# A two-layer decoder trunk on one Trainium2 core: the first weight pieces in halves, gains applied to the transposed x, and broadcasts and lambda sums later on GpSimd

## The chip, the cores and the metric

The kernel runs on one core of a Trainium2 chip. The metric is the device time of one execution in microseconds (us), as the median of several runs. Positions in a trace are us from the start of the profiled span. TensorE is called PE in the rows, VectorE DVE, ScalarE ACT, GpSimd POOL and SyncE SP.

## The reference

x has 256 rows of 1024 float32. Two layers, each a half-step FFN, a mixer, and a second half-step FFN, and a last RMSNorm:

```python
for l in range(2):
    x = x + 0.5 * swiglu(rmsnorm(x, norm_ffn1[l]), w1_gate[l], w1_up[l], w1_down[l])
    h = rmsnorm(x, norm_mix[l])
    dq, dk, dv, rq, rk, rv, rg = split(h @ w_in[l])
    lam = (exp(sum(lambda_q1[l] * lambda_k1[l])) - exp(sum(lambda_q2[l] * lambda_k2[l])) + lam_init)
    ...
    x = x + concat(o_diff, o_ret) @ w_out[l]
    x = x + 0.5 * swiglu(rmsnorm(x, norm_ffn2[l]), w2_gate[l], w2_up[l], w2_down[l])
return rmsnorm(x, norm_final)
```

Left out are `o_diff`, differential attention with `lam` (4 heads), and `o_ret`, retention (4 heads). `rmsnorm(x, g)` is x / sqrt(mean(x^2) + 1e-6) * g, `swiglu` is (silu(x @ gate) * (x @ up)) @ down with an inner width of 2816.

## The kernel before, in words

**Precision.** Every matmul of weights is done three times. A weight piece (128 x 2048 float32, 1 MB) is loaded into one of three `raw` slots. ScalarE rounds it into `w_hi` (`split_hi`, L329), VectorE takes the rest, raw minus `w_hi`, into `w_lo` (`split_lo`, L536); both have six slots. TensorE then adds hi*hi, hi*lo and lo*hi (`three`, L798 to L800). The activations are split in the same way (`xT_hi`, `xT_lo` for the transposed x).

**Entry of a block** (number q, seven in all, the last being the output). x is held in two row tiles of 128 rows, tt = 0 and 1. For each, VectorE adds the accumulators to x (`residual`, L569), multiplies by `gain` into `wide` (L572), TensorE transposes `wide` into the PSUM tiles `tp` (`enter_T`, L813), ScalarE copies them to `xT_hi` (L354), VectorE subtracts into `xT_lo` (L553). ScalarE also sums the squares (`squares`, L349), and GpSimd makes the factor `rstd` from them in two small steps (`entry`, L226 and L228). `rstd` is applied after the projection, so the projection doesn't wait for it. `gain` holds one norm's weights, broadcast to all partitions; GpSimd reloads it after each entry (`next_gain`, 0.5 MB).

**FFN.** Eleven steps of 256 columns. A step has two `up` calls (one for each row tile, 24 matmuls with gate and up side by side in `gu[tt]`) and two `down` calls, which run one step behind. Between them the hidden tile is turned by way of memory: ScalarE silu (L372), VectorE product with `rstd` (`hide`, L595), GpSimd copy that takes the 16-bit halves apart (`turn_out`, L246), a transposing DMA triggered by ScalarE (`turn`, L377), GpSimd copy back (`turn_back`, L252), ScalarE and VectorE split (L382, L553). `up` number e waits for `hidden_done` e - 1, since two PSUM tiles are used in turn.

**What sets the order.** Each engine runs a program written out by hand and waits on counting semaphores. ScalarE's in a step are these:

```python
silu(s_, 0, it, pos)
nxt(0)
turn(d, 0)
silu(s_, 1, it, pos)
nxt(1)
turn(d + 1, 1)
```

where `nxt` splits a piece and `turn` begins with a wait for `halves_done` of GpSimd's copy. SyncE issues the weight loads in order; a load waits until the piece three before has been split.

**The start.** SyncE loads the first half of x (L160) and the pieces from L173; ScalarE triggers the gain broadcast (L509); GpSimd makes the identity, issues five broadcasts (four lambda vectors L279, diff_subln L280), makes the tables `bias8` and `decay`, then the two factors. ScalarE triggers the load of the second half of x only once piece 0 has landed (`act.wait_ge(raw_loaded[0], 32)`, L514, L515), and splits pieces 0 and 1 after that. VectorE sums the lambda products (L767).

Of the kernel before, what the change touches and what calls it, by code (L numbers as in the profile page):

```python
# [21 lines left out]
P = 128  # L22
D, SEQ, DEPTH = 1024, 256, 2
TT = SEQ // P
KT = D // P
# [28 lines left out]
def build(nc, x_in, norm_ffn1, w1_gate, w1_up, w1_down, norm_mix, w_in, lam_q1, lam_k1, lam_q2, lam_k2,  # L54
          subln, w_out, norm_ffn2, w2_gate, w2_up, w2_down, norm_final, out):
    ctx = ExitStack()
    with ctx:
# [16 lines left out]
        gain = sb("gain", [P, D])  # L74
# [27 lines left out]
        dq_dk = wide  # L102

# [8 lines left out]
        def retT(h, a, b):  # L112
# [11 lines left out]
        gain0_loaded = sem("gain0_loaded")  # L124
# [6 lines left out]
        acc_ready, x_new, xg_ready, sq_done, rstd_done, xT_psum, xT_hi_done, xT_lo_done = (  # L131
            sem(n) for n in ("acc_ready", "x_new", "xg_ready", "sq_done", "rstd_done", "xT_psum", "xT_hi_done", "xT_lo_done"))
# [25 lines left out]
        def _(sp):  # L158
# [16 lines left out]
            def ffn(layer, base, wg, wu, wd):  # L175
# [5 lines left out]

                def load_down(it, pos, j):
                    load(layer, it, base + pos, [wd[layer, bass.ds(j * CH + k * P, P), :] for k in range(2)])

                load_gu(0, 0, 0)
# [33 lines left out]
        def _(pool):  # L219
            def load_gain(src):  # L220
                pool.dma_start(gain[:, :], src.partition_broadcast(P)).then_inc(gain_loaded, 16)

# [14 lines left out]

            def next_gain(q, src):
                pool.wait_ge(xg_ready, 4 * q + 4)
                load_gain(src)  # L240
# [46 lines left out]
            for h in range(HEADS):  # L287
                nc.gpsimd.tensor_scalar(bias8[:, h, :], bias8[:, h, :], -SLOPES[h] / SCALE, None, ALU.mult).then_inc(pool_steps, 1)
            pool.wait_ge(decay_exp, HEADS)
            nc.gpsimd.tensor_scalar(decay[:, :, :], decay[:, :, :], SCALE, None, ALU.mult).then_inc(pool_steps, 1)  # L290
            pool.wait_ge(pool_steps, 5 + HEADS + DEPTH)
            nc.gpsimd.affine_select(out=bias8[:, :, :], in_=bias8[:, :, :], compare_op=ALU.is_ge, fill=MASKED, base=P,
                                    pattern=[[0, HEADS], [-1, SEQ]], channel_multiplier=1).then_inc(consts_made, 1)
            nc.gpsimd.affine_select(out=decay[:, :, :], in_=decay[:, :, :], compare_op=ALU.is_ge, fill=0.0, base=0,
                                    pattern=[[0, HEADS], [1, SEQ]], channel_multiplier=-1).then_inc(consts_made, 1)
            for tt in range(TT):
                entry(0, tt)
            next_gain(0, norm_mix[0, :])

            def mixer_and_ffn2_entry(layer):  # L300
                for tt in range(TT):
                    entry(3 * layer + 1, tt)
                next_gain(3 * layer + 1, norm_ffn2[layer, :])
# [7 lines left out]
            for layer in range(DEPTH):  # L311
                if layer:
                    for tt in range(TT):
                        entry(3 * layer, tt)
                    next_gain(3 * layer, norm_mix[layer, :])
                ffn(layer, 0)
                mixer_and_ffn2_entry(layer)
                next_gain(3 * layer + 2, norm_ffn1[layer + 1, :] if layer < DEPTH - 1 else norm_final[:])
                ffn(layer, 1)
# [5 lines left out]
        def _(act):  # L325
# [4 lines left out]

            def ahead(layer, pos, some=range(AHEAD)):

                for p_ in some:
                    split_hi(layer, pos + p_)
# [9 lines left out]
            def squares(q, tt):  # L344
                if isinstance(q, int) and q == 0:
                    act.wait_ge(x_loaded[tt], 16)
                else:
                    act.wait_ge(x_new, 4 * (q - 1) + 2 * tt + 2)
                nc.scalar.activation(junk.bitcast(BF16)[:, tt * D:(tt + 1) * D], x[:, tt, :], ACT.Square, accum_out=ssq[:, tt:tt + 1]).then_inc(sq_done, 1)  # L349

            def xT_parts(q, tt):
                for half in range(2):
                    act.wait_ge(xT_psum, 4 * q + 2 * tt + half + 1)
                    nc.scalar.activation(xT_hi[:, 4 * half:4 * half + 4, tt * P:(tt + 1) * P],  # L354
                                         tp[half][:, :].rearrange("p (k n) -> p k n", k=4), ACT.Copy).then_inc(xT_hi_done, 1)
# [83 lines left out]
            def mixer(layer):  # L439
# [33 lines left out]
                act.wait_ge(lam_steps, 2 * DEPTH)  # L473
# [35 lines left out]
            act.dma_start(gain[:, :], norm_ffn1[0, :].partition_broadcast(P)).then_inc(gain0_loaded, 16)  # L509
# [7 lines left out]
            for tt in range(TT):  # L517
                squares(0, tt)
            xT_parts(0, 1)
            with act.Fori(0, DEPTH) as layer:  # L520
# [12 lines left out]
        def _(dve):  # L533
# [4 lines left out]

            def ahead(layer, pos, some=range(AHEAD)):

                for p_ in some:
                    split_lo(layer, pos + p_)
# [12 lines left out]
            def residual(q, tt, factor, used):  # L555

                if factor is None:
                    dve.wait_ge(x_loaded[tt], 16)
                    dve.wait_ge(gain0_loaded, 16)
                else:  # L560
                    dve.wait_ge(gain_loaded, 16 * q)
                for half in range(2):
                    cols = slice(half * 512, (half + 1) * 512)
                    if factor is not None:
                        if (tt, half) != (1, 1):
                            dve.wait_ge(acc_ready, 3 * (q - 1) + 2 * tt + half + 1)
                        else:
                            dve.wait_ge(slot_free, SLOTS + used)
                        nc.vector.scalar_tensor_tensor(x[:, tt, cols], acc[2 * tt + half][:, :], factor, x[:, tt, cols],  # L569
                                                       ALU.mult, ALU.add).then_inc(x_new, 1)  # L570
                        dve.wait_ge(x_new, 4 * (q - 1) + 2 * tt + half + 1)
                    nc.vector.tensor_tensor(wide[:, tt, cols], x[:, tt, cols], gain[:, cols], ALU.mult).then_inc(xg_ready, 1)  # L572

            def xT_parts(q, tt):
                for half in range(2):
                    dve.wait_ge(xT_hi_done, 4 * q + 2 * tt + half + 1)
                    ks = slice(4 * half, 4 * half + 4)
                    lo_of(xT_lo[:, ks, tt * P:(tt + 1) * P], tp[half][:, :].rearrange("p (k n) -> p k n", k=4),
                          xT_hi[:, ks, tt * P:(tt + 1) * P], xT_lo_done)

            def enter(q, factor, used):
                for tt in range(TT):
                    residual(q, tt, factor, used)
                    xT_parts(q, tt)
# [172 lines left out]
            residual(0, 0, None, 0)  # L757
            xT_parts(0, 0)
            ahead(0, 0)
            residual(0, 1, None, 0)  # L760
            xT_parts(0, 1)
            dve.wait_ge(lam_loaded, 16 * 5)

            for l in range(DEPTH):
                for m in range(2):
                    cols = slice(l * QK, (l + 1) * QK)
                    nc.vector.tensor_tensor_reduce(out=gate[:, 0, (2 * l + m) * QK:(2 * l + m + 1) * QK], in0=lams[:, 2 * m, cols],  # L767
                                                   in1=lams[:, 2 * m + 1, cols], scale=1.0, scalar=0.0, op0=ALU.mult, op1=ALU.add,
                                                   accum_out=lam_dot[:, 2 * l + m:2 * l + m + 1]).then_inc(lam_steps, 1)
            for l in range(DEPTH):  # L770
                nc.vector.tensor_scalar(gsub2[:, l, :], gsub2[:, l, :], 1.0 - LAM_INIT[l], None, ALU.mult).then_inc(lam_steps, 1)
            with dve.Fori(0, DEPTH) as layer:
                ffn(layer, 0, 0)
                dve.wait_ge(lam_steps, 3 * DEPTH)

                nc.vector.tensor_copy(gsub[:, :], gsub2[:, bass.ds(layer, 1), :].rearrange("p l n -> p (l n)")).then_inc(layer_vals, 1)
                enter(3 * layer + 1, 0.5, LP * layer + MIX0)
                mixer(layer)
                enter(3 * layer + 2, 1.0, LP * layer + FFN2)
                ffn(layer, 1, FFN2)  # L780
                with dve.If(layer < DEPTH - 1):
                    enter(3 * layer + 3, 0.5, LP * layer + LP)
            q = 3 * DEPTH
            for tt in range(TT):
                residual(q, tt, 0.5, LP * DEPTH)
            for tt in range(TT):
                dve.wait_ge(rstd_done, TT * q + tt + 1)
                dve.wait_ge(xg_ready, 4 * q + 2 * tt + 2)
# [261 lines left out]
```

## Time and profile before

| | |
|---|---|
| median of 3 runs | 977.25 us (976.73 to 977.7) |
| the profiled execution | 975.21 us |
| its span | 973.4 us |
| PE busy | 944.2 us, 97% |
| DVE, ACT, POOL busy | 557.0, 460.7, 195.0 us |
| granted clock, mean | 0.998 |
| read from memory | 177.08 MB |

The span is the profiled part of the execution, 1.8 us shorter than the execution's own time. Busy time of an engine is the time its instructions cover; a wait of an engine is the gap before an instruction, with the releaser that ended it. The start and the turns from one block to the next are the places where TensorE may stand.

### The profile page before, as it was taken

The numbers are of one execution on the slowest core, as the hardware profiler recorded it, in microseconds if no ns is written. First come the engines' busy times: TensorE is split into PE (matmuls) and PEld (weight loads), VectorE is DVE, ScalarE is ACT, GpSimd is POOL, SyncE is SP. The second block draws the span as 40 slices with busy tenths as digits, with TensorE's granted clock in tenths as the row PEclk, the third lists the DMA queues.
The fourth block names the chain that finished last, engine by engine and source line by source line (L and its number), as shares of the span: only waits on it lengthen the run. The fifth ranks groups of instructions, "written<-read, shape, count | busy, mean of one in ns | idle before, by whom it ended". The sixth has DMA issues, their size and how long they took to land.

```text
span 973.4 us, 13400 instructions
## 1 busy us (share of the span) xinstructions
PE 944.2 (97%) x4352; PEld 781.8 (80%) x4352; DVE 557.0 (57%) x628; ACT 460.7 (47%) x579; POOL 195.0 (20%) x233
## 2 busy tenths in 40 slices
PE   2999999999999999999989999999999999999996
PEld 2888888888888888888878888888888888888885
DVE  3555555665576565555645656466665756555554
ACT  4544444545574444444454444344656545444441
POOL 7133211100010323131013311210001024212210
PEclk9999999999999999999999999999999999999999
DMA  9787777546345786666638867665624646867641
GB/s 253 211 233 212 209 226 226 188 162 213 113 148 173 205 244 204 216 200 220 223 112 233 231 196 217 204 214 190 228 97 172 211 126 215 249 191 227 193 143 43
DMA packets 166699, 189.19 MB, mean 194 GB/s; under 512 B 49184, under 2 KB 139296, under 8 KB 166656
## 3 DMA queue, kind: packets, MB, share of 16 engines
q1 hardware_dynamic: 121808, 173.56, 54.3%
q10 hardware_dynamic: 43808, 11.54, 6.8%
q0 software_dynamic: 1040, 3.54, 1.3%
q8 instruction: 23, 0.38, 0.2%
q14 instruction: 20, 0.16, 0.1%
HBM read 177.08 MB, written 1.05 MB: 183 GB/s over the span
## 4 chain that ended last, share of the span: by engine, by line
PE 95%; DMA 1%; ACT 1%; DVE 1%; issue 1%; SPq 0%; ACTq 0%; POOLq 0%; DVEq 0%; POOL 0%
PE gu L798 21%; PE gu L800 21%; PE gu L799 21%; PE acc L800 10%; PE acc L798 10%; PE acc L799 10%; DMA raw<-in_w_up_dram 1%; PE tp L813 1%; PE tp L912 1%; PE acc L923 1%; PE tp L935 1%; DVE w_lo L536 0%; ACT w_hi L329 0%; ACT wide L452 0%; PE acc L935 0%
## 5 line engine op out<-in xcount | busy, mean ns | idle before, releaser
L536 DVE TENSOR_TENSOR w_lo<-raw,w_hi 128x2048 fp32r<-128x2048 f32 (+1 forms) x168 | 383.0, 2284 | 164.3 <-ACT w_hi L329 163.8
L798 PE MATMUL gu<-w_hi,xT_hi 128*128 128x512 f32 x896 | 352.4, 393 | 13.0 <-DVE w_lo L536 10.5
L800 PE MATMUL gu<-w_hi,xT_lo 128*128 128x512 f32 x896 | 349.5, 390 | 0.0
L799 PE MATMUL gu<-w_lo,xT_hi 128*128 128x512 f32 x896 | 349.5, 390 | 0.0
L329 ACT ACTIVATE w_hi<-raw 128x2048 fp32r<-128x2048 f32 (+1 forms) x168 | 313.0, 1867 | 21.6 <-DMA raw<-in_w_up_dram 10.9
L798 PEld LDWEIGHTS gu<-w_hi,xT_hi 128*128 128x128 f32 x896 | 168.7, 188 | 49.3 <-issue 12.9
L800 PEld LDWEIGHTS gu<-w_hi,xT_lo 128*128 128x128 f32 x896 | 168.6, 188 | 35.5
L799 PEld LDWEIGHTS gu<-w_lo,xT_hi 128*128 128x128 f32 x896 | 168.8, 188 | 34.2
L798 PE MATMUL acc<-w_hi,aT_hi 128*128 128x512 f32 x384 | 150.8, 393 | 0.0
L800 PE MATMUL acc<-w_hi,aT_lo 128*128 128x512 f32 x384 | 149.6, 390 | 0.0
L799 PE MATMUL acc<-w_lo,aT_hi 128*128 128x512 f32 x384 | 149.4, 389 | 0.0
L372 ACT ACTIVATE hid<-gu,st 128x256 f32<-128x256 f32 x88 | 41.6, 473 | 219.3 <-PE gu L800 186.9
L246 POOL COPY kT<-hid 128x512 uint16<-128x512 uint16 x80 | 60.6, 757 | 332.1 <-DVE hid L595 332.1
L252 POOL COPY qT<-kT 128x512 uint16<-128x512 uint16 x80 | 97.0, 1219 | 125.1 <-issue 88.3
L595 DVE SCALAR_TENSOR_TENSOR hid<-gu,st,hid 128x256 f32<-128x256 f32 x88 | 42.4, 482 | 123.2 <-ACT hid L372 123.1
L382 ACT ACTIVATE aT_hi<-qT 128x256 fp32r<-128x256 f32 x80 | 33.4, 417 | 133.4 <-POOL qT L252 133.4
L800 PEld LDWEIGHTS acc<-w_hi,aT_lo 128*128 128x128 f32 x384 | 72.1, 188 | 15.2
L799 PEld LDWEIGHTS acc<-w_lo,aT_hi 128*128 128x128 f32 x384 | 72.2, 188 | 14.7
L798 PEld LDWEIGHTS acc<-w_hi,aT_hi 128*128 128x128 f32 x384 | 72.1, 188 | 14.4
L553 DVE TENSOR_TENSOR aT_lo<-qT,aT_hi 128x256 fp32r<-128x256 f32 x80 | 35.0, 438 | 46.1 <-ACT aT_hi L382 46.1
L354 ACT ACTIVATE xT_hi<-tp 128x512 fp32r<-128x512 f32 x24 | 13.2, 596 | 61.0 <-PE tp L813 61.0
L226 POOL TENSOR_SCALAR st<-st 128x1 f32<-128x1 f32 x14 | 3.8, 274 | 179.3 <-ACT rT L349 179.2
(115 smaller groups left out, 406.8 us busy)
## 6 DMA issues: line engine op xcount, KB each, us to landing
raw<-in_w_gate_dram SPq DMA_DIRECT2D x88, 512.0 KB, 4.0
raw<-in_w_up_dram SPq DMA_DIRECT2D x88, 512.0 KB, 5.0
raw<-in_w_down_dram SPq DMA_DIRECT2D x88, 512.0 KB, 3.9
raw<-in_w_in_dram SPq DMA_DIRECT2D x40, 512.0 KB, 4.7
raw<-in_w_out_dram SPq DMA_DIRECT2D x16, 512.0 KB, 3.6
raw<-in_w_in_dram SPq DMA_DIRECT2D x16, 256.0 KB, 2.8
gain<-in_norm_ffn_dram POOLq DMA_DIRECT2D x3, 512.0 KB, 3.7
kT<-kT ACTq DMA_TRANSPOSE x80, 3.3
```

The lines of the kernel that those rows point to most:

```text
L246: nc.gpsimd.tensor_copy(halves[:, tt, :, :], hidden[:, tt, :].bitcast(U16).rearrange("p (n h) -> p h n", h=2)).then_inc(halves_done, 1)
L252: nc.gpsimd.tensor_copy(hidT[:, tt, :].bitcast(U16).rearrange("p (n h) -> p h n", h=2), halvesT[:, tt, :, :]).then_inc(hidT_done, 1)
L329: nc.scalar.activation(w_hi[:, pos % SLOTS, 0:n], raw[:, pos % RAW, 0:n], ACT.Copy).then_inc(hi_done, 1)
L354: nc.scalar.activation(xT_hi[:, 4 * half:4 * half + 4, tt * P:(tt + 1) * P], tp[half][:, :].rearrange("p (k n) -> p k n", k=4), ACT.Copy). ...
L372: nc.scalar.activation(silu_g[:, tt, :], gu[tt][:, 0:CH], ACT.Silu, scale=rstd[:, tt:tt + 1]).then_inc(silu_done, 1)
L382: nc.scalar.activation(aT_hi[:, 2 * par:2 * par + 2, tt * P:(tt + 1) * P], hidT[:, tt, :].rearrange("p (k n) -> p k n", k=2), ACT.Copy).th ...
L536: nc.vector.tensor_tensor(w_lo[:, pos % SLOTS, 0:n], raw[:, pos % RAW, 0:n], w_hi[:, pos % SLOTS, 0:n].bitcast(F32), ALU.subtract).then_in ...
L553: nc.vector.tensor_tensor(dst, src, hi.bitcast(F32), ALU.subtract).then_inc(done, 1)
L595: nc.vector.scalar_tensor_tensor(hidden[:, tt, :], gu[tt][:, CH:2 * CH], rstd[:, tt:tt + 1], silu_g[:, tt, :], ALU.mult, ALU.mult).then_in ...
L798: nc.tensor.matmul(out_, s_hi, m_hi, start=first, stop=False)
L799: nc.tensor.matmul(out_, s_hi, m_lo, start=False, stop=False)
L800: return nc.tensor.matmul(out_, s_lo, m_hi, start=False, stop=last)
```

## The change

- **Weights.** Pieces 0 and 1 of each layer's first FFN are loaded in two halves of 1024 columns (`load_first`), each with its own semaphore, and split in halves by ScalarE and VectorE (`split_first_hi`, `split_first_lo`). TensorE waits for `lo_half` ahead of the first two of a piece's four row blocks, for `lo_done` ahead of the third.
- **Gains.** The three norms' weights (two layers each) are loaded as 48 rows of 128 (24 KB), transposed once by TensorE, and kept as `gT`, one column for each 128 values. TensorE transposes x itself; VectorE multiplies the transposed tile in PSUM by `gT` into `wide`, and the hi and lo parts are made from `wide`. The output norm's gain alone is still a broadcast, into `gate`, loaded once.
- **GpSimd.** The five small broadcasts are issued after the two factors of the first entry. The lambda sums are made there by a product and six halving additions, and `gsub2` is scaled there.
- **ScalarE at the start.** The squares of row tile 1 come after its `xT_parts`.

```diff
+                def load_first():
+                    for pos in range(AHEAD):
+                        sp.wait_ge(lo_done, LP * layer + pos + 1)
+                        for part, loaded in enumerate((half_loaded, raw_loaded)):
...
+                            for g, w in enumerate((wg, wu)):
+                                rows = slice(pos * 512 + part * 256, pos * 512 + (part + 1) * 256)
+                                sp.dma_start(dst[:, :, g, :], w[layer, rows, 0:CH].rearrange("(k p) n -> p k n", p=P)).then_inc(loaded[pos], 16)
...
-            for i, lam in enumerate((lam_q1, lam_k1, lam_q2, lam_k2)):
-                pool.dma_start(lams[:, i, :], lam.rearrange("l n -> (l n)").partition_broadcast(P)).then_inc(lam_loaded, 16)
-            pool.dma_start(gsub2[:, :, :].rearrange("p l n -> p (l n)"),
-                           subln.rearrange("l n -> (l n)").partition_broadcast(P)).then_inc(lam_loaded, 16)
...
+            for tt in range(TT):
+                entry(0, tt)
+            for i, lam in enumerate((lam_q1, lam_k1, lam_q2, lam_k2)):
+                pool.dma_start(lams[:, i, :], lam.rearrange("l n -> (l n)").partition_broadcast(P)).then_inc(lam_loaded, 16)
...
+            pool.wait_ge(lam_loaded, 16 * 5)
+            pairs = lams.rearrange("p (m b) (l n) -> p m b l n", b=2, l=DEPTH)
+            dots = pairs[:, :, 0, :, :]
+            nc.gpsimd.tensor_tensor(dots, dots, pairs[:, :, 1, :, :], ALU.mult).then_inc(lam_sums, 1)
+            for i in range(6):
+                n = QK >> (i + 1)
+                dst = dots[:, :, :, 0:n] if n > 1 else lam_dot.rearrange("p (l m n) -> p m l n", m=2, n=1)
+                pool.wait_ge(lam_sums, i + 1)
+                nc.gpsimd.tensor_tensor(dst, dots[:, :, :, 0:n], dots[:, :, :, n:2 * n], ALU.add).then_inc(lam_sums, 1)
+            for l in range(DEPTH):
+                nc.gpsimd.tensor_scalar(gsub2[:, l, :], gsub2[:, l, :], 1.0 - LAM_INIT[l], None, ALU.mult).then_inc(lam_sums, 1)
...
+            def split_first_hi(layer, pos):
+                nth = layer + pos // LP
+                act.wait_ge(half_loaded[pos % LP], 32 * nth + 32)
+                act.wait_ge(slot_free, LP * layer + pos + 1)
+                nc.scalar.activation(w_hi[:, pos % SLOTS, 0:1024], raw[:, pos % RAW, 0:1024], ACT.Copy).then_inc(hi_half, 1)
+                act.wait_ge(raw_loaded[pos % RAW], 32 * (LP // RAW * layer + pos // RAW + 1))
+                nc.scalar.activation(w_hi[:, pos % SLOTS, 1024:PIECE], raw[:, pos % RAW, 1024:PIECE], ACT.Copy).then_inc(hi_done, 1)
...
-            act.dma_start(gain[:, :], norm_ffn1[0, :].partition_broadcast(P)).then_inc(gain0_loaded, 16)
+            for i, norm in enumerate((norm_ffn1, norm_mix, norm_ffn2)):
+                act.dma_start(gain_rows[i * DEPTH * KT:(i + 1) * DEPTH * KT, :],
+                              norm.rearrange("l (k p) -> (l k) p", p=P)).then_inc(gains_loaded, 16)
...
             act.wait_ge(raw_loaded[0], 32)
             act.dma_start(x[:, 1, :], x_in[0, P:2 * P, :]).then_inc(x_loaded[1], 16)
             ahead(0, 0)
-            for tt in range(TT):
-                squares(0, tt)
+            squares(0, 0)
             xT_parts(0, 1)
+            squares(0, 1)
...
+                for half in range(2):
+                    dve.wait_ge(xT_psum, 4 * q + 2 * tt + half + 1)
+                    g = gT[:, bass.ds(col + 4 * half, 4)].unsqueeze(2).broadcast_to([P, 4, P])
+                    nc.vector.tensor_tensor(of(wide, half), tp[half][:, :].rearrange("p (k n) -> p k n", k=4), g, ALU.mult).then_inc(xg_done, 1)
...
-                          xT_hi[:, ks, tt * P:(tt + 1) * P], xT_lo_done)
...
+                    lo_of(xT_lo[:, ks, tt * P:(tt + 1) * P], of(wide, half), xT_hi[:, ks, tt * P:(tt + 1) * P], xT_lo_done)
```

GpSimd's instructions from its first tables to its first copy of a hidden tile (`kT<-hid`), before:

```order
L279 DMA qT<-in_lambda_k_dram 128x128
L280 DMA gsub<-in_diff_subln_dram 128x256
L283 MEMSET st 128x1 x2
L284 IOTA bias 128x1024
L288 TENSOR_SCALAR bias<-bias 128x256 x4
L290 TENSOR_SCALAR decay<-decay 128x1024
L292 AFFINE_SELECT bias<-bias 128x1024
L294 AFFINE_SELECT decay<-decay 128x1024
L226 TENSOR_SCALAR st<-st 128x1
L228 TENSOR_TENSOR st<-st 128x1
```

The second factor, one reload of `gain` (L221) and the copy follow. And with the change, from the second factor's last step on:

```order
L242 TENSOR_TENSOR st<-st 128x1
L301 DMA qT<-in_lambda_q_dram 128x128
L301 DMA qT<-in_lambda_k_dram 128x128
L301 DMA qT<-in_lambda_q_dram 128x128
L301 DMA qT<-in_lambda_k_dram 128x128
L302 DMA gsub<-in_diff_subln_dram 128x256
L305 TENSOR_SCALAR decay<-decay 128x1024
L307 AFFINE_SELECT decay<-decay 128x1024
L312 TENSOR_TENSOR qT<-qT 128x2x128
L317 TENSOR_TENSOR qT<-qT 128x2x2x32
L317 TENSOR_TENSOR qT<-qT 128x2x2x16
L317 TENSOR_TENSOR qT<-qT 128x2x2x8
```

Three more additions, two TENSOR_SCALAR on `gsub2` and then the copy of the first hidden tile (L256) follow. The broadcasts and the work on `decay` moved from ahead of the factors to behind them, and the lambda steps joined them.

ScalarE at the start, before:

```order
L354 ACTIVATE xT_hi<-tp 128x4x128 x2
L515 DMA x<-in_x_dram 128x1024
L329 ACTIVATE w_hi<-raw 128x2048 x2
L349 ACTIVATE rT,st<-x 128x1024 x2
L354 ACTIVATE xT_hi<-tp 128x4x128 x2
```

And with the change:

```order
L386 ACTIVATE xT_hi<-wide 128x4x128 x2
L549 DMA x<-in_x_dram 128x1024
L356 ACTIVATE w_hi<-raw 128x1024
L358 ACTIVATE w_hi<-raw 128x1024
L356 ACTIVATE w_hi<-raw 128x1024
L358 ACTIVATE w_hi<-raw 128x1024
L381 ACTIVATE rT,st<-x 128x1024
L386 ACTIVATE xT_hi<-wide 128x4x128 x2
L381 ACTIVATE rT,st<-x 128x1024
```

The pieces are split in four halves, still behind the load of x's second half, and the second squares moved behind the copies of the second x tile.

## Rows read from the trace of the kernel before

**Rows 1.** Who waited for whom, TensorE: total us, times, longest.

```profile
PE gu L798 <- DVE w_lo L536: 10.5, 1, 10.5
PE tp L813 <- DVE wide L572: 7.3, 1, 7.3
```

**Rows 2.** The chain that ended last, 0 to 26 us: start, duration, what.

```profile
2.15 12.80 DMA raw<-in_w_up_dram
...
15.42 1.92 ACT w_hi L329
...
17.36 2.30 DVE w_lo L536
...
19.80 0.79 PE gu L798
...
24.57 0.87 PE tp L813 x8
```

**Rows 3.** Windows of the start: busy us by engine, clock, DMA share, GB/s.

```profile
0.00:7.00 7.00, 0.00 (x0) 0.00 (x0) 0.53 (x1) 2.62 (x5) 6.05 (x17) 1.00 0.68 214
7.00:15.00 8.00, 1.94 (x8) 1.55 (x8) 2.35 (x4) 1.19 (x2) 7.69 (x7) 1.00 0.96 178
15.00:20.00 5.00, 0.20 (x1) 0.21 (x2) 2.54 (x2) 4.10 (x3) 0.51 (x1) 1.00 1.10 368
```

**Rows 4.** DMA issues, 0 to 40 us: KB each, us from issue to landing.

```profile
x<-in_x_dram ACTq DMA_DIRECT2D x1, 512.0 KB, 7.0
...
gsub<-in_diff_subln_dram POOLq DMA_DIRECT2D x1, 128.0 KB, 10.1
```

**Rows 5.** Timeline, first x tile: start, us, engine, line, operation, [idle before].

```profile
6.47 1.49 DVE L572 TENSOR_TENSOR wide<-x,gain 128x512 f32<-128x512 f32 x2 [6.47 <-DMA x<-in_x_dram]
...
9.29 0.60 ACT L354 ACTIVATE xT_hi<-tp 128x512 fp32r<-128x512 f32 x1 [0.26 <-PE tp L813]
```

**Rows 6.** Timeline of ScalarE from its first table load in layer 1.

```profile
26.15 1.28 ACT L329 ACT_TABLE_LOAD   x1
...
30.68 0.48 ACT L372 ACTIVATE hid<-gu,st 128x256 f32<-128x256 f32 x1
```

**Rows 7.** Timeline of GpSimd, 0 to 36 us.

```profile
2.51 0.75 POOL L279 DMA_DIRECT2D qT<-in_lambda_q_dram  x1
...
4.87 0.55 POOL L280 DMA_DIRECT2D gsub<-in_diff_subln_dram  x1
...
10.52 2.77 POOL L290 TENSOR_SCALAR decay<-decay 128x1024 f32<-128x1024 f32 x1
...
14.46 1.05 POOL L294 TENSOR_SCALAR_AFFINE_SELECT decay<-decay 128x1024 f32<-128x1024 f32 x1
20.84 1.25 POOL L226 TENSOR_SCALAR st<-st 128x1 f32<-128x1 f32 x1 [5.33 <-ACT rT L349]
...
23.19 0.19 POOL L226 TENSOR_SCALAR st<-st 128x1 f32<-128x1 f32 x1
...
32.27 0.60 POOL L246 COPY kT<-hid 128x512 uint16<-128x512 uint16 x1 [7.69 <-DVE hid L595]
```

**Rows 8.** GpSimd's copy back, one line: ns min/median/max.

```profile
L252 POOL COPY qT<-kT x80: 757/770/2919, 38.2 to 941.6; 128x512 uint16<-128x512 uint16 x80
```

**Rows 9.** Groups by form, GpSimd: count, busy us, mean ns, idle before.

```profile
L288 POOL TENSOR_SCALAR bias<-bias 128x256 f32<-128x256 f32 x4 | 3.8, 949 | 0.2
...
L234 POOL TENSOR_SCALAR hn<-hn 128x4 f32<-128x4 f32 x8 | 1.5, 190 | 134.2 <-ACT rT L436 133.8
```

**Rows 10.** Timeline of TensorE: first matmuls of the fourth `up` and of `down`.

```profile
38.91 0.39 PE L798 MATMUL gu<-w_hi,xT_hi 128*128 128x512 f32 x1
...
44.35 0.39 PE L798 MATMUL acc<-w_hi,aT_hi 128*128 128x512 f32 x1
```

**Rows 11.** Timeline of TensorE at the start of layer 2.

```profile
506.38 0.49 PE L798 MATMUL gu<-w_hi,xT_hi 128*128 128x512 f32 x1 [0.74 <-DVE hid L595]
```

**Rows 12.** Timeline of VectorE at the end.

```profile
968.76 0.88 DVE L791 TENSOR_SCALAR x<-wide,st 128x512 f32<-128x512 f32 x2 [0.71 <-POOL st L228]
```

More of the change, by code:

```diff
@@ L537, in split_lo, with split_first_lo @@
                                         w_hi[:, pos % SLOTS, 0:n].bitcast(F32), ALU.subtract).then_inc(lo_done, 1)
+            def split_first_lo(layer, pos):
+                nth = layer + pos // LP
+                for part, when, count, done in ((0, hi_half, AHEAD * nth + pos % LP + 1, lo_half), (1, hi_done, LP * layer + pos + 1, lo_done)):
+                    cs = slice(part * 1024, (part + 1) * 1024)
+                    dve.wait_ge(when, count)
+                    nc.vector.tensor_tensor(w_lo[:, pos % SLOTS, cs], raw[:, pos % RAW, cs], w_hi[:, pos % SLOTS, cs].bitcast(F32),
+                                            ALU.subtract).then_inc(done, 1)
             def ahead(layer, pos, some=range(AHEAD)):
                 for p_ in some:
-                    split_lo(layer, pos + p_)
+                    if pos % LP:
+                        split_lo(layer, pos + p_)
+                    else:
+                        split_first_lo(layer, pos + p_)
             def ahead_after(layer, f, some):
@@ L785, in _ @@
                 residual(q, tt, 0.5, LP * DEPTH)
+                for half in range(2):
+                    cols = slice(half * 512, (half + 1) * 512)
+                    dve.wait_ge(gain_loaded, 16)
+                    dve.wait_ge(x_new, 4 * q + 2 * tt + half + 1)
+                    nc.vector.tensor_tensor(wide[:, tt, cols], x[:, tt, cols], gain[:, cols], ALU.mult).then_inc(xg_done, 1)
             for tt in range(TT):
                 dve.wait_ge(rstd_done, TT * q + tt + 1)
-                dve.wait_ge(xg_ready, 4 * q + 2 * tt + 2)
+                dve.wait_ge(xg_done, 4 * q + 2 * tt + 2)
                 for half in range(2):
@@ L807, in enter_T, with project @@
                 for half in range(2):
-                    pe.wait_ge(xg_ready, 4 * q + 2 * tt + half + 1)
+                    if isinstance(q, int) and q == 0:
+                        pe.wait_ge(x_loaded[tt], 16)
+                    else:
+                        pe.wait_ge(x_new, 4 * q + 2 * tt + half + 1)
                     if tt:
-                        pe.wait_ge(xT_lo_done, 4 * q + half + 1)
+                        pe.wait_ge(xg_done, 4 * q + half + 1)
                     for k in range(4):
                         c = (4 * half + k) * P
-                        ins = nc.tensor.transpose(tp[half][:, k * P:(k + 1) * P], wide[:, tt, c:c + P], ident[:, :])
+                        ins = nc.tensor.transpose(tp[half][:, k * P:(k + 1) * P], x[:, tt, c:c + P], ident[:, :])
                     ins.then_inc(xT_psum, 1)
-            def project(layer, it, tt, pos, n_pieces, ready, hook=None, entry=None):
+            def project(layer, it, tt, pos, n_pieces, ready, hook=None, entry=None, halved=False):
                 kk = KT // n_pieces
@@ L821, in project @@
                     slot = (pos + h) % SLOTS
-                    if tt == 0:
+                    if tt == 0 and halved:
+                        pe.wait_ge(lo_half, AHEAD * layer + h + 1)
+                    elif tt == 0:
                         piece_ready(layer, pos + h, it)
@@ L825, in project @@
                         kt = h * kk + k
+                        if halved and tt == 0 and k == 2:
+                            piece_ready(layer, pos + h, it)
                         if entry is not None and kt in (0, KT // 2):
@@ L861, in up @@
                         pe.wait_ge(hidden_done, e - 1)
-                    project(layer, it, tt, base + pos, 2, gu_ready, hook, entry)
+                    project(layer, it, tt, base + pos, 2, gu_ready, hook, entry, entry is not None and base == 0)
                 def hidden_T(e, tt):
```

115 lines of the change are left out of this document (57 added, 58 removed).

## The prediction

> **What bounds the kernel now.** I read the list of what TensorE waited for first, then the chain of waits of the first 26 us, then the start and the layer's turn engine by engine. The list has few entries [rows 1]: 10.5 us before the first weights, 7.3 us before the first x, little else; TensorE is busy for 97% of the span. So only the start, the turns between blocks and the end can move. The chain shows the start [rows 2]: the first piece of weights lands at 2.15 + 12.80 = 14.95 us, ScalarE makes its upper part until 17.34, VectorE its lower part until 19.66, and TensorE begins at 19.80. Its first 12 matmuls last until 24.57. The windows show why the piece is late [rows 3]: 214 GB/s for 7 us (1.5 MB: x, the gain's broadcast and a third of a piece or more), then 178 GB/s for 8 us although weights are queued, then 368. While it is slow, five small broadcasts of GpSimd are under way; the last took 10.1 us to land [rows 4].
>
> All positions below are us from the span's start; those after the change are my estimates.
>
> **The start after the change: 8.5 us gained.** Ahead of the first piece the queues hold x (0.5 MB) and 24 KB of gains in place of x, 0.5 MB of gain and 0.38 MB of broadcasts. x plus the piece are 1.5 MB, which is what the first 7 us moved [rows 3], so I put the piece at 7.2 plus an allowance of 0.6 for its completion: 7.8. The halves don't bring that forward: ScalarE still waits for the whole of piece 0 before it triggers the second half of x (L515), and only then splits. x itself, there at 6.47 before [rows 5] behind 0.5 MB of gain that are gone (1.4 us at 368 GB/s), comes at about 5.0; transposes, the moved multiply and the upper part follow. Before, multiply, transposes and both upper parts reached from 6.47 to 9.89 [rows 5]; with the multiply behind the transposes of each half I get 8.4. Then 0.45 for the trigger (14.95 to 15.42 before), half of 1.92 plus 0.1 for the first upper half, half of 2.30 plus 0.1 for its lower half, 0.1 for the wait: TensorE begins at 11.3 instead of 19.80. The transpose of the gain rows (48 columns) lies in the wait for x. The second half of x took 7.0 us before [rows 4]; triggered at 8.5 it is there by 15.5, and TensorE asks for it at 11.3 + 4.6 = 15.9. No stall, but no slack.
>
> **Behind it: 0.8 us returned.** TensorE wants piece 2 and the first hidden tile after two row tiles: at 38.91 - 5.44 = 33.47 before [rows 10], so 13.7 us in, now 25.0. ScalarE gets to its table load once it has copied the second x tile (26.15) before; now a multiply (0.7 twice, overlapped) and squares(0, 1) stand in front: squares end at 19.6. Table load, upper part of piece 2, table load and silu then take until 24.6 as they did from 26.15 to 31.16 [rows 6]. VectorE takes piece 2 from 22.9 to 25.2, then 0.5 for the hidden tile: 25.7, and with its gap 25.8.
>
> **GpSimd: 7.6 us returned.** This decides. Before, GpSimd was idle when the first hidden tile came, and copied it out at 32.27 [rows 7]. Now its queue holds, behind both entry factors (done at squares' end plus 1.0: 20.7), five DMA issues, one TENSOR_SCALAR on decay, an affine_select, seven lambda steps that each wait for the one before, two for gsub2, and only then the copy. Prices: issues 2.9 us (2.51 to 5.42), decay 2.77 plus 1.05 for the select [rows 7]; lambda steps have no row, their bounds are 190 ns (128x4) and 949 ns (128x256) [rows 9], so 1.3 to 6.6 for seven; as only the first has 256 elements and they halve, I take 3.2; gsub2 1.2. Sum 11.1: 31.8.
>
> To this come collisions. The first factor took 1.25 us while VectorE subtracted weights, the next 0.19 [rows 7]; the copies back range from 757 to 2919 ns [rows 8]. I read this as GpSimd standing still while VectorE subtracts two SBUF tiles. VectorE's subtraction of piece 2 (22.9 to 25.2) holds back decay by 1.6, and that of piece 3 fits in behind decay: 2.3 more. So the copy starts at 35.7. The Trainium skill ("SBUF — State Buffer", Who interferes with whom) states this as a rule: a VectorE instruction with two SBUF inputs contends with a GpSimd one that reads SBUF, and whoever comes second is blocked for the whole instruction. By that rule the trace agrees (0.19 against 1.25); without it the copy would start at 31.8.
>
> ScalarE waits for this copy (halves_done) before it triggers the transposing DMA, and its silu of the second row tile stands behind. From the copy's start to TensorE's fourth `up`: copy 0.6, trigger 1.3, silu 0.5, hide 0.5, and gaps, together 3.1. So `up` number four starts at 38.8, where it started at 38.91 before [rows 10]: of the 7.7 us gained, 7.6 are gone. TensorE has finished the third `up` at about 33 (25.8 + 5.44, and 1.8 inside it for piece 3, whose subtraction waits for decay to end at 28) and stands for 6 us.
>
> **TensorE's speed after it: 1.7 us lost.** The first 12 matmuls after the wait of 10.5 us took 4.77 us [rows 2]; 24 later ones take 5.44 [rows 10], so 12 would take 2.7. The spacing tells the level, 1.2 instead of 2.4 GHz. A short restart costs 0.2 to 0.3 anyway, which leaves 1.7 if 6 us of standing bring the low level back. At nothing otherwise.
>
> **Start of layer 2: 1.0 us lost.** The turn's second half has no slack: TensorE waits 0.74 for the hidden tile [rows 11]. With the multiply between transposes and upper part, ScalarE's copies, its squares and all behind them begin later: 0.69 + 0.05 for the first, another 0.25 because the second multiply paces them. The other turns (two mixers, two second FFNs) have the same 1.0 us more on ScalarE, but TensorE had no wait there; I cost them at nothing, hidden by the rest of the first block (5.4 us per row tile); if that cover is gone it is 0.1 to 0.5 each.
>
> **The end, and edits with no price.** The last multiply comes after both residual halves; VectorE stood idle 0.71 us before the last pair [rows 12], which covers it. Gains no longer reloaded, six lambda operations off VectorE: all idle time elsewhere.
>
> **Sum.** -8.5 + 0.8 + 7.6 + 1.7 + 1.0 = +2.6. The profiled execution took 975.21 us; the median is 2.04 above it. 975.21 + 2.6 + 2.04 = 979.85, so 979.9.
>
> **Rivals.** A measurement of this kernel can't tell less than 0.2% (1.95 us) from nothing.
> 1. *GpSimd's queue is shorter* (lambda steps near 190 ns, one collision or none): the copy starts at 31.5 to 33, TensorE stands 2 to 3 us and stays fast. The fourth `up` starts 2.8 to 4.3 earlier than before, less 1.0: 974 to 975.5, and 973.5 to 976.5 with the first piece half a us either way. For it: the steps are tiny. Against: the subtractions fall where the queue is. It decides once the copy starts before 34.8 with fast matmuls, 33.1 with slow ones.
> 2. *GpSimd's queue doesn't reach TensorE*: 8.5 - 0.8 - 1.0 = 6.7 gained, 970.5. It needs the queue empty by 28.1, 7.6 us earlier than I have it; the issues, decay and select alone end at 27.4.
> 3. *The broadcasts land late*: the last took 10.1 us. Issued at 23.1 it lands at 33.2, after the select, and the lambda steps start then: copy at 37.6, 982 or, if the first piece is 1 us later too, 983.
> 4. *The first piece isn't earlier than 10*, because the dip to 178 GB/s has another cause than the broadcasts: 2 to 4 us more than the forecast, 982 to 984.
>
> **Numbers.** Forecast 0.45 (977.5 to 981.5), rival 1 0.25, rival 2 0.10, rival 3 0.13, rival 4 0.07. Below 975.3 lie rival 2 and some 0.18 of rival 1: faster 0.28. Slower by more than 1.95 (above 979.2) are rivals 3 and 4 and over half of the forecast: 0.44. Same 0.28. The range 972.5 to 982.5 leaves out rival 2 and the outer parts of 3 and 4.
>
> **What would show it.** First matmul near 11.3; a wait of TensorE of 5 to 7 us near 33 that ends with VectorE's hidden tile, and before it GpSimd without idle time from 20 to 36; slow matmuls behind it; 1.7 us in place of 0.74 at the start of layer 2. I am wrong if GpSimd copies the first hidden tile before 30, if the lambda steps take under 1.5 us together, or if the first piece lands after 10.

## The result and the profile after

| | before | after |
|---|---|---|
| median (16 runs each, taken together) | 976.09 us (973.86 to 978.65) | 980.52 us (978.44 to 982.34) |
| the profiled execution | 975.21 us | 979.55 us |
| its span | 973.4 us | 977.7 us |
| granted clock, mean | 0.998 | 0.993 |

The changed kernel takes 1.0045 times as long, with a 95% interval of 1.0036 to 1.0054: slower by 4.4 us. The two profiled executions stand 4.3 us apart, so their traces can be set side by side.

What TensorE waited for in the profile after (total us, times, longest) answers to [rows 1]:

```profile
PE gu L841 <- DVE hid L638: 8.1, 3, 5.8
PE gu L1075 <- DMA rv<-in_norm_ffn_dram: 5.3, 1, 5.3
PE gu L841 <- DVE w_lo L578: 3.7, 1, 3.7
```

The 10.5 us ahead of the first weights have become 3.7. The first wait of the kernel, 7.3 us for the first x before, is now 5.3 us for the gain rows. And the waits for VectorE's hidden tile, 0.74 us before [rows 11], have grown to 8.1 us in three pieces. These are the three, with the first matmul, in TensorE's timeline (start, duration, operation, the wait before it):

```profile
11.24 0.79 PE L841 MATMUL gu<-w_hi,xT_hi 128*128 128x512 f32 x1 [3.74 <-DVE w_lo L578]
...
25.90 0.49 PE L841 MATMUL gu<-w_hi,xT_hi 128*128 128x512 f32 x1 [0.50 <-DVE hid L638]
...
37.84 0.80 PE L841 MATMUL gu<-w_hi,xT_hi 128*128 128x512 f32 x1 [5.81 <-DVE hid L638]
38.43 0.63 PE L842 MATMUL gu<-w_lo,xT_hi 128*128 128x512 f32 x1
38.86 0.63 PE L843 MATMUL gu<-w_hi,xT_lo 128*128 128x512 f32 x1
...
510.06 0.49 PE L841 MATMUL gu<-w_hi,xT_hi 128*128 128x512 f32 x1 [1.82 <-DVE hid L638]
```

The first matmul is 8.56 us earlier than in [rows 2]; the fourth `up` (37.84) is only 1.07 us earlier than in [rows 10]. Its matmuls then come 0.43 us apart, the spacing of the 1.2 GHz level, until 43.1. The windows of the same trace (busy us by engine, PEclk, DMA share, GB/s) show both ends of this:

```profile
7.00:15.00 8.00, 4.26 (x12) 3.10 (x11) 7.10 (x8) 6.09 (x8) 2.28 (x4) 1.00 1.08 358
15.00:20.00 5.00, 5.00 (x26) 4.17 (x25) 2.58 (x4) 2.43 (x5) 0.31 (x2) 1.00 0.99 357
20.00:30.00 10.00, 9.39 (x40) 7.16 (x39) 4.98 (x3) 6.59 (x5) 9.71 (x9) 1.00 0.68 75
30.00:40.00 10.00, 4.19 (x14) 3.10 (x14) 1.38 (x2) 2.35 (x3) 5.30 (x12) 0.81 0.64 197
```

The dip to 178 GB/s of [rows 3] is gone (358 in the same stretch). From 30 to 40 us TensorE is busy for 4.19 us, and the granted clock is 0.81. (The clock column doesn't show every slow stretch: from 11.8 to 15.2 us the matmuls are 0.43 us apart too, and it reads 1.00. At the start the spacing tells the level.)

**Who holds the hidden tile.** GpSimd's timeline from the end of the first entry to its first copy; [rows 7] show the same copy after 7.69 us of idle time:

```profile
20.18 0.56 POOL L242 TENSOR_TENSOR st<-st 128x1 f32<-128x1 f32 x1
20.69 0.79 POOL L301 DMA_DIRECT2D qT<-in_lambda_q_dram  x1
...
23.09 0.55 POOL L302 DMA_DIRECT2D gsub<-in_diff_subln_dram  x1
23.66 4.36 POOL L305 TENSOR_SCALAR decay<-decay 128x1024 f32<-128x1024 f32 x1
28.09 1.80 POOL L307 TENSOR_SCALAR_AFFINE_SELECT decay<-decay 128x1024 f32<-128x1024 f32 x1
30.77 0.74 POOL L312 TENSOR_TENSOR qT<-qT 128x256 f32<-128x256 f32 x1 [0.88 <-DMA gsub<-in_diff_subln_dram]
31.59 1.77 POOL L317 TENSOR_TENSOR qT<-qT 128x128 f32<-128x128 f32 x5
33.45 0.20 POOL L317 TENSOR_TENSOR st<-qT 128x4 f32<-128x4 f32 x1
33.61 1.14 POOL L319 TENSOR_SCALAR gsub<-gsub 128x128 f32<-128x128 f32 x2
34.69 0.61 POOL L256 COPY kT<-hid 128x512 uint16<-128x512 uint16 x1
```

VectorE made that tile between two subtractions of weights (its timeline):

```profile
23.08 2.29 DVE L570 TENSOR_TENSOR w_lo<-raw,w_hi 128x2048 fp32r<-128x2048 f32 x1 [3.58 <-ACT w_hi L350]
25.29 0.48 DVE L638 SCALAR_TENSOR_TENSOR hid<-gu,st,hid 128x256 f32<-128x256 f32 x1
26.67 2.29 DVE L570 TENSOR_TENSOR w_lo<-raw,w_hi 128x2048 fp32r<-128x2048 f32 x1 [0.90 <-ACT w_hi L350]
```

It was ready at 25.77. It lay for 8.9 us while GpSimd worked for nobody who was waiting. ScalarE stood behind it, since its program has the transposing DMA, which needs the copy, ahead of the silu of the second row tile:

```profile
35.40 1.28 ACTq L409 DMA_TRANSPOSE kT<-kT  x1
36.79 0.47 ACT L404 ACTIVATE hid<-gu,st 128x256 f32<-128x256 f32 x1 [10.16 <-issue]
```

The row names "issue" as what ended its 10.16 us; the semaphore that it stood at is read from the program (`halves_done` in `turn`), and the end of the copy at 35.3 fits it.

**The ledger**, each position after minus the same before:

| place | after minus before | step |
|---|---|---|
| first matmul | 11.24 - 19.80 = -8.56 | -8.56 |
| third `up` | 25.90 - 33.47 = -7.57 | +0.99 |
| fourth `up` | 37.84 - 38.91 = -1.07 | +6.50 |
| first `down` | 45.85 - 44.35 = +1.50 | +2.57 |
| last transposes ahead of layer 2's first `up` | 490.66 - 488.20 = +2.46 | +0.96 |
| transposes in layer 2's first `up` pair | 499.03 - 496.43 = +2.60 | +0.14 |
| third `up` of layer 2 | 510.06 - 506.38 = +3.68 | +1.08 |
| mixer's entry in layer 2 | 678.26 - 673.69 = +4.57 | +0.89 |
| last transposes | 967.05 - 961.98 = +5.07 | +0.50 |
| end of the span | 977.7 - 973.4 = +4.3 | -0.77 |

(33.47 is the prediction's 38.91 - 5.44, and the trace has the row.) By 46 us all of the earlier start is gone and 1.5 us more. From there to the last transposes another 3.6 us come, and the end gives 0.8 back. The ledger sets one execution beside one other, and executions of one kernel differ by up to 4.8 us here, so its steps under 1 us are shown for these two alone.

### The profile page after: what moved, and what is told of

It reads as the page before. It is cut to its first block, busy times and chain, and to the rows that moved or that the text cites. A ratio compares the mean times of both kernels' runs of the same rounds, so it can differ in the third digit from the quotient of the medians.

```text
span 977.7 us, 13427 instructions
## 1 busy us (share of the span) xinstructions
PE 950.2 (97%) x4353; PEld 784.7 (80%) x4353; DVE 556.1 (57%) x623; ACT 463.4 (47%) x583; POOL 197.2 (20%) x237
## 3 DMA queue, kind: packets, MB, share of 16 engines
HBM read 173.96 MB, written 1.05 MB: 179 GB/s over the span
## 4 chain that ended last, share of the span: by engine, by line
PE 92%; DMA 2%; ACT 2%; issue 1%; POOL 1%; DVE 1%; ACTq 0%; POOLq 0%; DVEq 0%
PE gu L841 20%; PE gu L843 20%; PE gu L842 20%; PE acc L841 10%; PE acc L843 10%; PE acc L842 10%; PE tp L859 1%; PE tp L962 1%; DMA kT<-kT 1%; DMA gsub<-in_diff_subln_dram 1%; PE acc L973 1%; PE tp L985 1%; ACT rT L381 0%; ACT w_hi L350 0%; ACT wide L484 0%
## 5 line engine op out<-in xcount | busy, mean ns | idle before, releaser
L570 DVE TENSOR_TENSOR w_lo<-raw,w_hi 128x2048 fp32r<-128x2048 f32 (+1 forms) x164 | 374.3, 2286 | 163.3 <-ACT w_hi L350 162.9
L350 ACT ACTIVATE w_hi<-raw 128x2048 fp32r<-128x2048 f32 (+1 forms) x164 | 305.5, 1867 | 15.5 <-DMA raw<-in_w_in_dram 8.4
L262 POOL COPY qT<-kT 128x512 uint16<-128x512 uint16 x80 | 105.0, 1314 | 121.1 <-issue 99.7
L256 POOL COPY kT<-hid 128x512 uint16<-128x512 uint16 x80 | 53.1, 663 | 329.4 <-DVE hid L638 329.4
L386 ACT ACTIVATE xT_hi<-wide 128x512 fp32r<-128x512 f32 x24 | 14.8, 632 | 64.0 <-DVE wide L618 63.8
```

What stands on the lines that cost most here:

```text
L256: nc.gpsimd.tensor_copy(halves[:, tt, :, :], hidden[:, tt, :].bitcast(U16).rearrange("p (n h) -> p h n", h=2)).then_inc(halves_done, 1)
L262: nc.gpsimd.tensor_copy(hidT[:, tt, :].bitcast(U16).rearrange("p (n h) -> p h n", h=2), halvesT[:, tt, :, :]).then_inc(hidT_done, 1)
L350: nc.scalar.activation(w_hi[:, pos % SLOTS, 0:n], raw[:, pos % RAW, 0:n], ACT.Copy).then_inc(hi_done, 1)
L570: nc.vector.tensor_tensor(w_lo[:, pos % SLOTS, 0:n], raw[:, pos % RAW, 0:n], w_hi[:, pos % SLOTS, 0:n].bitcast(F32), ALU.subtract).then_in ...
```

## The experiments

My theory after the result: the gain of 8.6 us is real, GpSimd's queue takes it back by way of the first hidden tile, and the low level of the clock adds to it. The rivals: the fourth `up` was late for weights or a table; the turn at layer 2 is ScalarE's squares.

**Stand-ins.** Every experiment has plain copies in place of the transposing DMAs of the hidden tile: the same bytes, triggered in the same place, not transposed. This part of the computation is left out in all of them, the two stand-ins included; no edit was run on the kernels with the transposing DMAs:

```diff
-   ..., halves[:, tt, :, :].rearrange("p h n -> p (h n)"), transpose=True)
+   ..., halves[:, tt, :, :].rearrange("p h (k n) -> p (h k) n", k=2))
```

v0_before is the kernel before with this edit:

> The kernel before with one thing left out: the DMA between GpSimd's two copies moves the hidden tile without transposing it (same bytes, same queue and order). It is the ground on which the parts of the change are compared. Its trigger should take ScalarE some 0.4 us in place of 1.2, and the turn was not on TensorE's path before, so every theory expects the time of the kernel before within 1 us, 975 to 977.

Measured: 975.53 us (974.45 to 977.0), 0.9993 of the kernel before [0.9983, 1.0002]. v0_after is the changed kernel with it:

> The changed kernel with the same thing left out. Theory (GpSimd's queue holds the first hidden tile's copy, ScalarE waits for it, silu of tile 1 stands behind): first copy of a hidden tile near 34.7 us, and TensorE's wait before the fourth `up` only 0.9 us shorter than the 5.8 of the change, because the trigger is shorter; slow matmuls behind it; 3 to 4 us above the kernel before with plain copies. Rival (the transposing DMA itself was what took the time): the wait falls by 2 us or more and the two are within 1 us.

Measured: 976.48 us (975.86 to 977.93), 0.9996 [0.9987, 1.0006]. The stand-in of the kernel before is a good one. That of the changed kernel is faster than its original by more than expected: the two are 0.95 us apart by their medians, not 4.4, where I had expected 3 to 4. The rival's total came true, but not its reason: the wait ahead of the fourth `up` fell by only 0.68 us, to 5.13. Its trace has the same shape, and one of the differences:

```profile
34.45 0.61 POOL L256 COPY kT<-hid 128x512 uint16<-128x512 uint16 x1
```

```profile
35.17 0.51 ACTq L409 DMA_DIRECT2D kT<-kT  x1
35.80 0.47 ACT L404 ACTIVATE hid<-gu,st 128x256 f32<-128x256 f32 x1 [9.49 <-POOL kT L256]
```

(v0_after, GpSimd's and ScalarE's timelines.) A plain DMA takes ScalarE's queue 0.51 us instead of 1.28, and the fourth `up` starts at 36.84 instead of 37.84. That explains 1 us. Part of the rest is the draw: the profiled execution of v0_after is the slowest of its eleven (977.93), 3.0 us over the profiled one of v0_before. Of the 3.5 us between the two differences (4.4 and 0.95) 1 is explained, and I leave 2.5 open. So the stand-ins show where the time goes and not the whole of the 4.4 us. Experiments are compared with v0_after, and the main conclusion rests on a step of over 7 us.

**GpSimd's long steps behind the first FFN** (w1_queue_late): decay, lambda steps and the scaling of `gsub2` (diff_subln's weights; the expectations call them gain rows) are issued once the first FFN's copies are; the broadcasts stay. What the expectation calls the first half of K is the first hidden tile, which GpSimd copies into `kT`.

```diff
-            pool.wait_ge(decay_exp, HEADS)
-            ...
+            def tables_and_lambda():
+                pool.wait_ge(decay_exp, HEADS)
+                ...
                 ffn(layer, 0)
+                if layer == 0:
+                    tables_and_lambda()
                 mixer_and_ffn2_entry(layer)
```

> The changed kernel with the plain copies, in which GpSimd's decay table, lambda steps and scaling of the gain rows stand behind the first FFN (the five broadcasts stay where the change put them); compared with v0_after, 976.5 us. My theory, that the queue of GpSimd takes back what the earlier start gives: the copy of the first half of K comes near 25 us instead of 34.5, TensorE's 5.1 us wait ahead of the fourth `up` and the matmuls at the slow level behind it are gone, and the time is 970 to 972 us, 5 to 7 us less than v0_after. A wait at layer 2's first turn (1.8 us) stays. The rival, that the fourth `up` was late for its weight piece or for the activation's table: the wait moves to another name and under 3 us are gained, 974 us or more.

Measured: 969.23 us (968.77 to 969.89), 0.9913 of the kernel before [0.9898, 0.9927]: 7.3 us under v0_after by the medians, 8.1 by the two ratios (0.0083 x 977), a little more than the 5 to 7 that I expected. TensorE's waits of w1_queue_late:

```profile
PE gu L1078 <- DMA rv<-in_norm_ffn_dram: 5.4, 1, 5.4
PE gu L844 <- DVE w_lo L581: 3.7, 1, 3.7
PE gu L844 <- DVE hid L641: 2.2, 2, 1.7
```

and the copy in GpSimd's timeline:

```profile
22.71 0.55 POOL L302 DMA_DIRECT2D gsub<-in_diff_subln_dram  x1
25.58 0.61 POOL L256 COPY kT<-hid 128x512 uint16<-128x512 uint16 x1 [2.32 <-DVE hid L641]
```

The copy follows the tile at once, and of the 5.1 us ahead of the fourth `up` nothing is left (a wait of 0.46 us ahead of the first `down` is new). The clock:

```profile
30.00:40.00 10.00, 9.54 (x43) 7.55 (x42) 3.43 (x5) 3.00 (x4) 2.14 (x3) 1.00 0.88 308
```

It stays at 1.00 in the window in which v0_after has 0.77. Set beside v0_after's, the trace is 5.3 us earlier at the fourth `up` (31.51 for 36.84) and 7.4 earlier at the first `down` (37.57 for 44.95). So the queue, and with it the slow stretch, is the cause of the lost gain; weights and tables are not. The wait at layer 2 (1.71 of the 2.2 us) stays, as it should.

**Squares first, too** (w2_queue_late_squares), as w1_queue_late with this, and with both squares ahead of the second `xT_parts` at the program's start:

```diff
-                    xT_parts(q, tt)
                     squares(q, tt)
+                    xT_parts(q, tt)
```

> As w1_queue_late, and ScalarE takes the squares of the new x before it splits the transposed x, at each layer's start and at the program's. My theory, that the turn into a layer is longer because the splits of xT now stand ahead of the squares and the table load on ScalarE: the wait ahead of the third `up` of layer 2 falls from 1.8 to under 0.8 us, the 0.5 us wait ahead of the program's third `up` goes, and the time is 1 to 2 us below w1_queue_late. The rival, that the gains' place in the transposed x sets it (the chain through `wide`, not ScalarE's order): the waits stay and the two times are within 0.4 us.

Measured: 968.59 us (966.77 to 970.1), 0.9901 [0.9884, 0.9918]. That is 0.6 us below w1_queue_late with overlapping intervals, where the theory wanted 1 to 2 and the rival at most 0.4; the total doesn't decide. The small wait ahead of the program's third `up` did go, but the one at layer 2 did not (1.79 us): the rival holds there. The parts of that turn, from the timelines of the kernel before,

```profile
497.06 1.09 ACT L354 ACTIVATE xT_hi<-tp 128x512 fp32r<-128x512 f32 x2 [6.11 <-PE tp L813]
498.03 1.06 ACT L349 ACTIVATE rT<-x 128x1024 bf16<-128x1024 f32 x1
...
500.32 1.28 ACT L329 ACT_TABLE_LOAD   x1 [1.14 <-issue]
```

of the changed kernel (VectorE's row, then ScalarE's),

```profile
499.67 1.29 DVE L618 TENSOR_TENSOR wide<-tp,gT 128x512 f32<-128x512 f32 x2 [4.38 <-PE tp L859]
```

```profile
500.39 1.23 ACT L386 ACTIVATE xT_hi<-wide 128x512 fp32r<-128x512 f32 x2 [5.99 <-DVE wide L618]
501.53 1.04 ACT L381 ACTIVATE rT<-x 128x1024 bf16<-128x1024 f32 x1
...
504.00 1.28 ACT L350 ACT_TABLE_LOAD   x1 [1.34 <-issue]
```

and of w2_queue_late_squares:

```profile
492.65 1.23 ACT L389 ACTIVATE xT_hi<-wide 128x512 fp32r<-128x512 f32 x2 [5.78 <-DVE wide L621]
496.23 1.28 ACT L353 ACT_TABLE_LOAD   x1 [2.35 <-issue]
```

The multiply puts 500.39 - 499.67 = 0.72 us between transposes and upper part. From the upper part's start to the table load it is 3.26 us before, 3.61 after, and 3.58 in w2_queue_late_squares, where the squares are long done: ScalarE then has 2.35 us without work instead of 1.04 of squares. From the table load to the third `up` it is 6.06 in all three. So in these two executions 0.72 + 0.35 make the 1.08 of the ledger, and the squares are no part of it. The 0.35 need not be the change's: v0_after, with the order of the changed kernel, has 3.29 us for the same stretch and w1_queue_late 3.49. What paces the 3.3 to 3.6 us is open; a loop's jump lies there. Leaving the multiply out, the direct test, was not tried.

**The broadcasts at their old place** (w3_bcast_early): the changed kernel with the five broadcasts ahead of the tables.

```diff
+            for i, lam in enumerate((lam_q1, lam_k1, lam_q2, lam_k2)):
+                pool.dma_start(lams[:, i, :], ...)
+            pool.dma_start(gsub2...)
             for l in range(DEPTH):
                 nc.gpsimd.memset(neg_init[:, l:l + 1], -LAM_INIT[l]).then_inc(pool_steps, 1)
```

> The changed kernel with the plain copies, but the five broadcasts of lambda vectors and gain rows issued where the kernel before issued them, ahead of the entry's work. My theory, that the early start comes half from the broadcasts' leaving the first weight loads alone: the first matmul starts at 14 us or later instead of 11.35; GpSimd's queue has no issues and no wait for the broadcast any more, so the copy comes some 3.5 us earlier, and the time stands within 1.5 us of v0_after (975 to 978). The rival, that the first piece is early for its size alone: first matmul by 12.3 us, and the time 2.5 us or more below v0_after.

Measured: 977.05 us (974.84 to 979.67), 0.9994 [0.9981, 1.0007]. The first matmul is at 13.80, 2.45 us later than in v0_after, just short of the 14 I gave and well past the rival's 12.3. The window shows the old dip again, deeper:

```profile
7.00:15.00 8.00, 2.00 (x7) 1.41 (x6) 5.36 (x6) 3.26 (x4) 4.03 (x5) 1.00 0.97 151
```

151 GB/s against 341 in v0_after, with a DMA share near 1.0 in both. So moving the broadcasts is worth 2.45 us at the first matmul. The total came as expected, but not its reason: GpSimd's copy came later, at 36.99, not 3.5 us earlier. The last half piece landed only at 19.1, ScalarE's first squares stood behind its split until 21, and the factors came at 25.6 instead of 20.4; the queue behind them then has no issues and no wait, and still ends later: it is 11.4 us long instead of 14.1, but begins 5.2 us later. Its select took 2.73 us and its first five sums 3.70, against 1.80 and 1.77 in v0_after, under the next subtractions of VectorE. The total is the same because one delay took the place of another.

**Whole pieces** (w4_whole_pieces): as w1_queue_late, with loads and splits of 2048 columns as in the kernel before.

```diff
-                if base == 0:
-                    load_first()
-                else:
-                    load_gu(0, 0, 0)
+                load_gu(0, 0, 0)
```

> As w1_queue_late, but the first three weight pieces are loaded and split whole, as in the kernel before. My theory: the first matmul starts near 13.2 us instead of 11.35 and the time is 1.5 to 2.5 us above w1_queue_late, since nothing else waits before layer 1. The rival, that a whole piece comes as early, or that the third piece sets the pace anyway: within 0.5 us of w1_queue_late.

Measured: 972.26 us (970.99 to 973.55), 0.994 [0.9925, 0.9956], 3.0 us above w1_queue_late. ScalarE's first splits, of w4_whole_pieces and then of w1_queue_late:

```profile
9.54 1.89 ACT L350 ACTIVATE w_hi<-raw 128x2048 fp32r<-128x2048 f32 x1
```

```profile
8.96 1.04 ACT L359 ACTIVATE w_hi<-raw 128x1024 fp32r<-128x1024 f32 x1
```

The first matmul is at 13.90 against 11.39: 0.58 from a later start of the split, 0.85 from the upper part, 1.08 from the lower and its hand-over. In both runs the chain to that start goes through the gain rows, whose DMA took 4.14 us here and 3.57 there, not through the piece. The piece alone would have made part of the difference, though: whole, it landed at 8.8, its two halves at 7.9. 2.5 of the 3.0 us stand there already, and with the queue out of the way they reach the end.

## Why the prediction was right, and where not

979.9 us was predicted and 980.52 measured, beside a kernel before that took 976.09 in the same series, 1.16 less than the median predicted from. In terms of the change itself, +2.6 us was predicted and +4.3 (traces) or +4.4 (medians) measured. The main case held. The closeness of the two times is in part luck: the lower time of the kernel before hides 1.2 of the 1.8 us by which the change was priced too low.

- **The start, -8.5:** -8.56. The split of the first half began at 8.80 (8.4 + 0.45 predicted). w3 and w4 show two of its parts, each alone: 2.45 for the broadcasts, 2.5 for the halves. What the 0.5 MB of gain gave was not tried. One sentence was wrong: "The transpose of the gain rows (48 columns) lies in the wait for x." The chain of the changed kernel at the start:

```profile
1.75 3.41 DMA rv<-in_norm_ffn_dram
...
5.29 0.31 PE gu L1075
5.60 1.92 PE tp L859 x8
...
8.27 0.37 ACT xT_hi L386
...
8.81 1.04 ACT w_hi L356
```

  The 24 KB, issued as three DMAs, landed 3.41 us after the last issue, and TensorE waited for them until 5.29. x had been there at 4.4 (0.88 plus 3.5 from issue to landing), not at 5.0 as predicted. So the gain rows, not x, start the chain, and they, not the piece, set the first matmul: the last part of piece 0 had landed at 8.1 (3.21 plus 4.9), just before ScalarE got to its trigger. It cost some 0.2 us here, since the piece would have held the trigger (8.27) until 8.1, and up to 0.5 in w1_queue_late (8.43 and 7.9). That two misses (x early, gain rows late) nearly cancelled is luck.
- **Behind it, +0.8:** +0.99; the third `up` at 25.90 for 25.8.
- **GpSimd, +7.6:** +6.50. The mechanism and place are confirmed by w1_queue_late. Its size was off by 1.1 us, the copy at 34.69 for 35.7. Issues 2.95 (2.9), lambda steps 2.88 (3.2), scaling 1.14 (1.2) were near. The two errors: "collisions" were put at 3.9 and measured (4.36 - 2.77) + (1.80 - 1.05) = 2.34; and rival 3, the late broadcast, took 0.88, which the forecast had at nothing. The last broadcast took 7.6 us to land, not 10.1, and came 0.9 us after the select's end: the queue and the landing were two paths of nearly the same length, and shortening decay alone should therefore gain little (argued from these rows, not tried).
- **Piece 3's subtraction "waits for decay to end":** wrong. It began at 26.67 as soon as ScalarE had made its upper part, with decay running until 28.02, and took its usual 2.29. The stop inside the third `up` was 0.3 us instead of 1.8. TensorE was through with it by 32.0, not 33, and so stood as long as predicted (5.81 for 6) though the fourth `up` came 1 us earlier.
- **The slow level, +1.7:** +2.57. The 24 matmuls from the fourth `up` to `down` took 8.01 us for 5.44, all of it on the slow spacing. I had taken the restart's 0.2 to 0.3 off and priced 12 matmuls by the first twelve's 4.77 us; here they took 43.11 - 37.84 = 5.27.
- **Layer 2, +1.0:** +1.08, but for a partly wrong reason: "its squares and all behind them begin later" put ScalarE's squares in the chain, and w2_queue_late_squares shows that they are not.
- **"The other turns ... I cost them at nothing":** this is the step that failed. The ledger has +0.96 up to layer 2 and +0.50 behind the mixer's entry in it. Of the first, one wait is visible (0.42 us, `acc` for `aT_lo` at 334.92, none before; the traces are 0.8 us further apart behind it than ahead of it); v0_after has no such wait, and where the rest comes from is open. And behind layer 2's turn the clock fell: seven or eight matmuls at 0.43 us spacing, 1.5 us while it lasted and +0.89 by the mixer's entry, which I had as possible for 6 us of standing but not for 1.8. Together 2.35 us, less 0.77 at the end. Of the changed kernel's 16 runs eight have a granted clock of 0.993 (981.0 us in the mean) and seven 0.995 (979.9). A stretch of 3.4 us at half the clock is 0.17% of the span, so I estimate from these numbers that about half of the runs had one like it, as the profiled one did.

The end's -0.77 was not foreseen either: from VectorE's last step to the end of the span it is 3.76 us before and 2.80 after, in which only the output's stores run.

## What to carry to other kernels

When a start is made earlier, walk each in-order queue from the new start to the first thing that a consumer waits for: work that had been hidden in a wait (here 9 us of tables and sums on GpSimd) is now in the path, and it is the place of that work, not the work, that costs. Move such work behind the first hand-over in its queue; here that kept the earlier start, and with the plain copies the time fell from 0.9996 to 0.9913 of the kernel before. And add the clock's price to any wait of TensorE that you create, as one of 1.8 us was followed by a slow stretch here.

## What the runs showed of the hardware

- **The clock falls after short waits, not always.** After the 1.82 us of waiting at 510.06 in the changed kernel, the fourth matmul shows it:

```profile
510.98 0.63 PE L841 MATMUL gu<-w_hi,xT_hi 128*128 128x512 f32 x1
511.41 0.63 PE L842 MATMUL gu<-w_lo,xT_hi 128*128 128x512 f32 x1
```

  The window 510 to 520 has a granted clock of 0.83. In w1_queue_late waits of 1.87 us at the turn before and of 1.71 us at the same place were followed by none, in v0_after the slow stretch came one turn earlier, behind 2.09 us. Of the six traced versions with the change five have one such stretch at these two turns; the kernel before and its stand-in, with waits of 1.6 and 0.7 to 0.9 us there, have none. What decides between them these runs don't show.
- **A VectorE subtraction holds up GpSimd's work that starts under it; the other way round it depends.** Decay began at 23.66 under one subtraction (23.08 to 25.37) and took 4.36 us for 2.77: from 25.37 it needed 2.65 us more. The next subtraction began at 26.67 under decay and neither was slowed; v0_after and w3_bcast_early show the same, at 26.34 and 27.95. The select, begun under that subtraction at 28.09 with 0.87 us of it left, took 0.75 more. But under GpSimd's copies VectorE is held too. In the kernel before (VectorE's, then GpSimd's timeline):

```profile
403.48 2.83 DVE L536 TENSOR_TENSOR w_lo<-raw,w_hi 128x2048 fp32r<-128x2048 f32 x1 [0.46 <-ACT w_hi L329]
```

```profile
403.46 0.76 POOL L252 COPY qT<-kT 128x512 uint16<-128x512 uint16 x1 [2.89 <-issue]
```

  The subtraction took 0.54 us more than its 2.29, with 0.74 of the copy left when it began. The Trainium skill ("SBUF — State Buffer", Who interferes with whom) has it that with two SBUF inputs on VectorE and reads on GpSimd the second to issue is blocked until the first has finished. By that rule decay and the select agree, and the subtraction under the copy nearly does. The subtraction under decay doesn't, since VectorE, second there, lost nothing. Why the two differ these runs don't show.
- **Small broadcasts take far more of the DMA than their bytes.** With 0.38 MB of them under way the core moved 151 GB/s between 7 and 15 us, without them 341, at a DMA share near 1.0 both times.
